# Prompt attention of one layer: scores made already turned, row maxima from rough scores ahead of them, and a new order at the edge between pairs of heads

## The reference, cut to what matters

```
q, k, v, f = split(rmsnorm(x) @ w_in)          # 16 heads of 64
q, k = rmsnorm per head (q, k); lf = log_sigmoid(f + b_f)
c = cumsum(lf)                                 # per head, over past and new frames
s = q @ k.T / 8 + c_q - c_k                    # masked to k_pos <= q_pos
attn = softmax(s) @ v                          # fp32
```

## Time and profile before

| | us |
|---|---|
| median of three runs | 2732.37 |
| the profiled execution | 2734.04 |
| its span, first to last instruction | 2732.4 |
| PE, DVE, ACT, POOL busy | 2316.4, 1336.0, 1020.5, 169.6 |
| attention: first projection to first score | 100.3 to 163.3 |
| attention: pairs 1 to 7 of 8 | 163.3 to 1018.6 |
| attention: last pair | 1018.6 to 1124.6 |

### The profile page before, as it was taken

The page is one execution under the profiler, slowest core; times in us unless marked ns, Lnnn a source line. Parts: engine busy times, 40 slices in busy tenths (PEclk is TensorE's granted clock), DMA queues, the critical chain, the costliest instruction groups (busy, mean ns, idle before and its releaser), DMA issues. The chain is left out here.

```text
span 2732.4 us, 37076 instructions
## 1 busy us (share of the span) xinstructions
PE 2316.4 (85%) x12096; PEld 1849.0 (68%) x12096; DVE 1336.0 (49%) x1639; ACT 1020.5 (37%) x1315; POOL 169.6 (6%) x175
## 2 busy tenths in 40 slices
PE   4678979898997989799899949989908999999991
PEld 2666858676776866699878849975505766666660
DVE  5345453545455453311255542212136888788874
ACT  3133222323323222211156632101106777777760
POOL 0111010101001000000011100000020000000002
PEclk9789999899989996799999979999958999999995
DMA  3210211302020110211245542133037999999986
GB/s 93 61 40 18 63 32 47 79 0 79 0 79 14 42 53 3 97 46 46 82 151 184 160 142 66 38 138 107 0 131 272 386 372 370 373 365 377 372 313 226
DMA packets 206037, 376.83 MB, mean 138 GB/s; under 512 B 19377, under 2 KB 127193, under 8 KB 205945
## 3 DMA queue, kind: packets, MB, share of 16 engines
q1 hardware_dynamic: 184776, 302.27, 32.7%
q0 software_dynamic: 17600, 61.18, 7.0%
q10 hardware_dynamic: 3584, 12.58, 1.2%
HBM read 301.60 MB, written 74.39 MB: 138 GB/s over the span
## 5 line engine op out<-in xcount | busy, mean ns | idle before, releaser
L1854 DVE TENSOR_TENSOR e_w_lo<-e_raw,e_w_hi 128x2048 fp32r<-128x2048 f32 x192 | 437.6, 2290 | 113.4 <-ACT e_w_hi L1781 101.0
L1781 ACT CAST e_w_hi<-e_raw 128x2048 fp32r<-128x2048 f32 x192 | 366.7, 1912 | 132.9 <-DMA e_raw<-w_down_e 53.5
L1154 ACT ACTIVATE probs_s<-scores,neg_max 128x256 f32<-128x256 f32 (+7 forms) x128 | 95.0, 742 | 446.4 <-DVEq L84 446.0
L1254 DVE COPY probsT<-turn_ps 128x512 f32<-128x512 f32 (+4 forms) x232 | 131.5, 567 | 249.1 <-PE turn_ps L1024 225.7
L101 PE MATMUL proj_ps<-w_qkv_hi,xh 128*128 128x384 f32 x544 | 194.5, 358 | 9.3 <-PEq L285 9.3
L1044 PEld LDWEIGHTS out_ps<-v_new,probsT 128*128 128x128 f32 x1152 | 160.1, 210 | 60.8 <-DVEq L84 44.3
L1044 PE MATMUL out_ps<-v_new,probsT 128*128 128x64 f32 x1152 | 180.6, 298 | 20.2 <-DVEq L84 19.0
L103 PE MATMUL proj_ps<-w_qkv_hi,xl 128*128 128x384 f32 x544 | 184.8, 340 | 0.0
L102 PE MATMUL proj_ps<-w_qkv_lo,xh 128*128 128x384 f32 x544 | 184.6, 339 | 0.0
L1240 DVE TENSOR_REDUCE neg_max<-scores 128x1 f32<-128x256 f32 (+7 forms) x128 | 97.0, 758 | 150.5 <-PE scores L1002 120.0
L1000 PE MATMUL scores<-qkT 65*128 65x512 f32 (+3 forms) x384 | 160.6, 532 | 5.8 <-DVEq L84 4.9
(11 more groups left out here) (363 smaller groups left out, 4967.1 us busy)
## 6 DMA issues: line engine op xcount, KB each, us to landing
e_raw<-w_gate_e SPq DMA_DIRECT2D x64, 1024.0 KB, 13.8
e_raw<-w_up_e SPq DMA_DIRECT2D x64, 1024.0 KB, 14.1
e_raw<-w_down_e SPq DMA_DIRECT2D x64, 1024.0 KB, 13.0
slot_x<-zrows POOLq DMA_DIRECT2D x48, 440.0 KB, 6.3
e_x<-slot_x SPq DMA_DIRECT2D x33, 384.0 KB, 11.1
w_qkv<-w_in SPq DMA_DIRECT2D x24, 512.0 KB, 10.0
slot_y<-e_y ACTq DMA_DIRECT2D x32, 384.0 KB, 6.2
slot_y<-zrows POOLq DMA_DIRECT2D x24, 352.0 KB, 9.6
```

The costliest lines, as they stand in the source:

```text
L1154: chain(sc.activation(probs[n % 2][:, 0:w], half(n)[:, 0:w], ACT.Exp, bias=neg_max[:, n:n + 1], accum_out=total[:, n:n + 1]), exp_ready)
L1254: chain(v.tensor_copy(probsT[q % 2][0:rows, 0:len(js) * P], turn_ps[0:rows, m % 2, 0:len(js) * P]), turn_taken[m % 2])
L1781: sc.copy(w_hi[u][:, :], w.raw[c][:, :]).then_inc(wh_ready, 1)
L1854: v.tensor_tensor(w_lo[u][:, :], w.raw[c][:, :], w_hi[u][:, :], ALU.subtract).then_inc(wl_ready, 1)
```

## The change

What it does, part by part:

- Scores of the prompt are made with keys on the partitions and 512 queries as the moving side, so they need no turning. There are four units (two heads, two halves of the queries) with 4, 8, 4 and 8 tiles of keys, together 24 steps (STEPS). A score is two fp32r matmuls into one bank: q and k rounded to fp32r, with three more rows for -c and the query's maximum (67 rows), and a second one of the two cross terms stacked to 128 rows.
- The exponential of a step is one ACT instruction of up to 512 columns straight into the moving side of the weighing. The values are stationary, with 64 columns of ones beside them, so the sum of the probabilities comes out of the same matmul on the other 64 partitions. DVE takes a reciprocal of 64x512 and one product for each unit.
- The row maximum now comes from rough scores, the first of the fp32r terms alone, in 24 chunks (MAXES) that all use one bank. PE turns the 128x3 results into rows by matmuls with the identity as the moving side, and ACT copies them behind q. The maxima of unit 0 of the next pair are taken at the edge.
- q and k are turned two tiles at a time, both heads in one transpose, in five groups. ACT writes the rounded part and a copy of k's, DVE the differences, and POOL copies q's rounded part.
- Past keys are turned for both heads at once, four times in place of eight, at steps 18 to 21. Weights are loaded and split in three parts with two raw buffers, at steps 18 and 22. The square root stands at step 19, the three parts of the normalization at 20 to 22. All of these stand ahead of the stream's scores.
- At the edge all five groups of q and k come first on every engine, then the stream's exponential, then its probabilities, with the four maximum chunks between them (EDGE).
- `forget_gates` also splits -c into two fp32r rows, and stores them with a row of ones.
- Nearly every wait inside the loops is followed by `alone`.

```diff
+    UNITS = [(0, 0), (0, 1), (1, 0), (1, 1)]
+    STEPS = [(u, j) for u in range(4) for j in range(4 * (UNITS[u][1] + 1))]
...
+    HALVES = 2 * NT
+    MAX_AT = {0: (4, 5, 6, 7), 1: (8, 9, 10, 11), 5: (12,), 6: (13,), 7: (14,), 8: (15,),
+              9: (16, 17), 10: (18, 19), 11: (20, 21), 12: (22, 23)}
+    ROWS_AT = {2: 1, 9: 2, 13: 3}
...
+    EDGE = (("qk", 0), ("qk", 1), ("qk", 2), ("qk", 3), ("qk", 4), ("p", 0), ("max", 0), ("p", 1), ("weigh", 0), ("max", 1),
+            ("weigh", 1), ("max", 2), ("p", 2), ("max", 3), ("weigh", 2), ("p", 3), ("rows", 0), ("weigh", 3), ("p", 4), ("weigh", 4))
...
+                def max_chunk(n):
+                    u, t, c0 = MAXES[n]
...
+                    last = te.matmul(max_ps[:, 0:w], high[0:HD + 2, h, 0, t * P:(t + 1) * P], high[0:HD + 2, h, 1, c0:c0 + w],
+                                     start=True, stop=not diagonal)
...
-                        for c0 in range(0, (t + 1) * P, BANK):
-                            w = min(BANK, (t + 1) * P - c0)
-                            diagonal = c0 + w == (t + 1) * P
-                            te.matmul(half(n)[:, c0:c0 + w], qkT[:, h, t * P:(t + 1) * P], qkT[:, 2 + h, c0:c0 + w],
-                                      start=True, stop=not diagonal)
...
+                        te.matmul(out[:, 0:q1 - q0], high[0:HD + 3, h, 1, j * P:(j + 1) * P], high[0:HD + 3, h, 0, q0:q1],
+                                  start=True, stop=False)
+                        last = te.matmul(out[:, 0:q1 - q0], cross[:, h, 1, j * P:(j + 1) * P], cross[:, h, 0, q0:q1],
+                                         start=False, stop=not diagonal)
...
+                        te.matmul(out_ps[u % 2][:, q0 - c * BANK:BANK], v_one[:, j, h, :], probsT[s % 2][:, 0:q1 - q0],
+                                  start=(j == 0), stop=(s == last_step(u)), skip_group_check=True).then_inc(pv_done, 1)
...
+                        def some_max():
+                            if maxes:
+                                n = maxes.pop(0)
+                                pe.wait_ge(max_taken, i * NM + n)
+                                alone(pe, g)
+                                max_chunk(n)
...
+                        some_max()
+                        some_max()
+                        if ahead and s < HALVES:
+                            project_half(s // 2, s % 2, proj_ps)
+                        some_max()
...
+                def take_cross(chain, p, b, bank):
+                    dve.wait_ge(high_ready, p * BATCHES + b + 1)
...
+                            chain(v.tensor_tensor(halves(cross[into, h, z, cols]), by_z[:, z, :, :], halves(high[0:HD, h, z, cols]),
+                                                  ALU.subtract), turn_taken[bank] if h and z else None)
...
+                        chain(v.reciprocal(recip[mine, :], out_ps[u % 2][other, :]))
+                        chain(v.tensor_tensor(out_T[mine, c * BANK:(c + 1) * BANK], out_ps[u % 2][mine, :], recip[mine, :], ALU.mult), out_taken)
```

More of the change, by code:

```diff
@@ L1101, in _ @@
+                    pe.wait_ge(out_taken, i * 5 + 5)
+                    alone(pe, g)
+                    bank = bank_of("o", 0)
+                    te.transpose(turn_ps[:, bank, 0:P], o_s, g.ident[:, :]).then_inc(turned, 1)
                 with pe.Fori(0, PAIRS - 1) as i:
@@ L1134, in _ @@
+                ones.then_inc(ones_ready, 1)
                 for t in range(NT):
[L1135 removed]
+                    take_tile(0, t, (proj_ps, out_ps[1])[t % 2], first=True)
                 root(0)
[L1137 to L1141 removed]
+                for b in range(BATCHES):
+                    act.wait_ge(turned, b + 1)
+                    alone(act, g)
+                    take_qk(b, b % 2)
@@ new lines, in past @@
+                    def past(c):
+                        m = use["past", c]
+                        act.wait_ge(turned, turned_count(i, m))
+                        alone(act, g)
+                        for h in range(2):
+                            last = sc.copy(kT_past[0:HD, h, c * BANK:(c + 1) * BANK], turn_ps[rows_of(h), m % 2, :])
+                            if h == 0:
+                                last.then_inc(chain_a, 1)
+                        last.then_inc(turn_taken[m % 2], 1)
@@ L1177, in step @@
-                    if ahead:
-                        root(i + 1)
-                        if more:
-                            round_w(i + 2)
-                        chain(sc.activation(warm[:, :], g.ident[:, 0:1], ACT.Exp))
-                        for t in range(TAKE_QK_ACT):
-                            m = use["qk", t]
-                            act.wait_ge(turned, turned_count(i, m))
-                            take_qk(chain, t, m % 2)
-                    exp(STREAM)
-                    if ahead:
-                        chain.ended(A_STEPS)
+                            alone(act, g)
@@ new lines, in step, with soft_stream @@
+                        if ahead and s == ROOT_AT:
+                            root(i + 1)
+                            sc.activation(warm[:, :], g.ident[:, 0:1], ACT.Exp).then_inc(chain_a, 1)
+                        if more and s in W_AT:
+                            for n in W_AT[s]:
+                                round_w(i + 2, n)
+                    def soft_stream():
+                        act.wait_ge(max_ready, i + 1)
+                        alone(act, g)
+                        sc.activation(probs_s, scores[:, :], ACT.Exp, bias=neg_max[:, 0:1], accum_out=total[:, 0:1]).then_inc(chain_a, 1)
+                        sc.activation(probs_tail[:, :], tail, ACT.Exp, bias=neg_max[:, 0:1], accum_out=total[:, 1:2]).then_inc(soft_ready, 1)
@@ L1191, in _ @@
+                    if not ahead:
+                        soft_stream()
+                        return
+                    for b in range(BATCHES):
+                        m = use["qk", b]
+                        act.wait_ge(turned, turned_count(i, m))
+                        alone(act, g)
+                        take_qk(b, m % 2)
+                    soft_stream()
+                    rows(0, i + 1)
                 with act.Fori(0, PAIRS - 2) as i:
@@ L1230, in _ @@
                     norm_part(chain, 0, s)
+                for b in range(BATCHES):
+                    take_cross(chain, 0, b, b % 2)
+                for n in range(U0_MAXES):
+                    maximum(chain, 0, n)
                 chain.ended(V_FIRST)
@@ new lines, in take_probs @@
+                        chain(v.tensor_copy(probsT[q % 2][0:rows, 0:n], turn_ps[0:rows, m % 2, 0:n]), turn_taken[m % 2])
+                    for s in range(NS):
+                        for n in MAX_AT.get(s, ()):
+                            maximum(chain, i, n)
+                        if s and STEPS[s - 1][0] != STEPS[s][0]:
+                            take_out(STEPS[s - 1][0])
+                        if ahead and s < HALVES and s % 2:
+                            sum_squares(chain, i + 1, s // 2)
+                        if ahead and s == HALVES - 1:
+                            mean(chain)
+                        if ahead and s in NORM_AT:
+                            norm_part(chain, i + 1, NORM_AT[s])
```

750 lines of the change are left out of this document (443 added, 307 removed).

## The result

The changed kernel took 2851.2 us (median of 4 runs, 2815.1 to 2865.1), the kernel before 2738.7 on the same chips (2718.8 to 2755.0). The ratio is 1.033 with a 95% interval of 1.018 to 1.048: slower, though the interval does not leave out a loss of under 2%. The profiled execution has a span of 2839.7 us, 107.3 more than before.

A forecast was written before the change was run, and what follows sets the result against it. The prediction took PE's work to bound the body and an ACT and DVE chain the edge. Pairs -16.5, start +7 and last pair -20 gave -29.5; from 2734.0, less 1.7 to the median, 2703 us, range 2646 to 2762.

The forecast's parts named there:

- The body, its clock: Body of each pair, up to the last projection: work priced at full clock, 73.5 us in all, against 83.3 before.
- The body, its work: PE's matmuls in a body, priced from the nearest rows of the old trace: 62.6 us.
- The body, its waits: PE's waits in a body: 7.5 for chunks sharing a bank, 0.8 for rows, 1.6 for tile copies, 1.0 for semaphores.
- The edge: From a pair's last projection to the next pair: 46.0 us, 2.5 of it for the clock, against 37.9; bounds 41 to 51.
- Six steps... ACT must clear them: At the edge's start: the last unit's six steps queue on ACT, ending near 13 us after the last projection.
- Rival 2: The edge eats the body's gain: a serial chain leaves PE at half clock; +26 us, 2758; chance 0.22.
- Rival 1: The clock holds in the pairs: edge 42, pair 115, last pair 70 us; -78 us, 2654; chance 0.27.
- Rival 3: POOL's copies hold DVE at the edge: 3.3 us a pair, 23 more than forecast, 2727; chance 0.06.
- Ahead of the pairs: Before the first score: later gates and half-clock batches, less a normalization stall; net +7 us, bounds 3 to 11.
- The last pair: Last pair of heads, without projections beneath it: 86 us instead of 106, so -20 us, bounds -42 to 0.
- Transposes and the clock: In the edge's last phase: old rows show the clock rising within transposes; by the skill's rule the edge nears 49 us.
- 2.3 us in seven pairs: Gain of each pair, 119.5 us instead of 121.8, forecast as -16.5 us over seven pairs.

The follow-up runs named there:

- e11: Changed kernel plus five useless fp32r matmuls at each of six places per body where two maximum chunks stand back to back; 2812.3 us.
- e14: e12's idea, stream's exponential after two q and k groups, third weight cast after ScalarE's first probability copy, more filler before weighings and rows; 2698.4 us, ratio 0.988.
- e2: e4 plus useless filler matmuls on TensorE in steps 21 to 23 and in the edge; 2810.7 us.
- e6: Changed kernel with maximum chunks spread through the projections, unit 3's output taken early as in e4, and e2's filler in the edge; 2732.3 us, ratio 1.001.
- e4: Changed kernel with VectorE taking unit 3's output before the stream's maxima instead of behind the subtractions; 2809.8 us.
- e8: e7 with the casts of the next weights moved out of ScalarE's queue ahead of the stream's scores; 2742.6 us, ratio 1.005.
- e12: e9 with the stream's sum of totals and its reciprocal moved behind the first copy of probabilities; 2718.3 us, ratio 0.994.
- e9: e6 with later weight casts as in e8, more filler ahead of the stream's scores, and filler in the last pair's waits; 2731.6 us, ratio 0.998.
- e7: e6 with the next pair's four maximum chunks between the q and k groups, giving up filler where they took its bank; 2754.8 us, ratio 1.012.
- e3: Changed kernel with the edge order undone: stream's exponential, probabilities and weighings first, then q and k, then maxima and rows; 2859.9 us.

## Why the prediction was wrong

- **The body, its clock: the step that failed.** "Body: 62.6 + 7.5 + 0.8 + 1.6 + 1.0 = 73.5 us" prices all at full clock. I had foretold each 1.05 us stall and asked only what it lasts, and had let the half clock of the edge end with the edge; what it costs the body stood at nothing, without a reason. Some 13 us of the second body run at half speed, half of them handed on by the edge, half from stalls on: 5 to 7 us lost, 3.9 of it shown by e11. It is one of three terms of like size. The 20.4 us by which a pair was missed are, within 0.4: this clock 6, the body's work 6.4, its waits -1.5, the edge's chain 7.7, the edge's clock 1.4.
- **The body, its work: mis-sized.** 62.6 us forecast; e14's body, at a clock of 1.00, has PE busy for 69.05. By starts of matmuls in it, projections take 40.1 (37.5 forecast), scores, masks and weighings 20.6 (18.2), chunks 5.5 (4.3), row matmuls 2.9 (2.6). The first matmul behind another kind comes after more than its pitch (0.31 us between the two halves of a score at 340.14, where 512 columns at the projections' rate give 0.23), and the new body changes kind 124 times. So rates from runs of equal matmuls came out as a lower bound for this mixed stream.
- **The body, its waits: right.** 10.9 us forecast, 9.4 measured, the 1.04 us stalls and ScalarE's tile copies among them. Sum: 69 + 9.4 + 6 = 84.4, measured 84.0 in this body.
- **The edge: mis-sized in the clock and in the chain.** "I take +2.5 of 7: edge 46.0". Measured 55.1. The clock is worth 3.9 by e2 (5.3 with what it hands to the next body, by e6). The rest is chain, read from the rows of one edge and only in parts tried by a run (e4, e8, e12): ScalarE's four casts for a batch take 1.95 us where I took 1.6, the scores start 0.9 later, and from unit 3's output to the next pair it was 15.9 us where I took 11 at full clock. "Six steps... ACT must clear them" and unit 3's reciprocal on the path were right (e4: 2.5).
- **Rival 2 was the right mechanism**, with 0.22: ScalarE's queue, half clock behind it, "at 51.5 a pair is 125". It lacked that the body pays the clock too, so even its 2758 was 93 short. Rival 1 (the clock holds) fell. Its argument, that the body had kept 0.99, read a property of the old instruction stream as one of the chip.
- **Rival 3:** the copies on GpSimd held nothing, the subtractions took 1.79 us all through. Its subtraction of two SBUF operands did: the first multiply took 1.34 us instead of 0.96 at 410.66, and e9's sum 2.25.
- **Ahead of the pairs:** +11.8 for +7. Normalization (done at 153.2 instead of 155.1) and the batches (10.9 us for 11) were right; the four maxima took 7.8 us instead of 4, four full round trips at half clock.
- **The last pair:** -19.1 for -20, right in sum by luck. I had divided 43 us of work by a clock of 0.61 and added 20 of waits, "all at full clock 64". The clock was 0.76, and at the full one the pair does not come near 64: 84.2 at 0.96 in e9 and 82.1 at 1.00 in e12, after 86.5 at 0.78 in e6. The clock is worth 2 to 4 us there, and what stands beside the 43 us of work is far more than 21.
- **Transposes and the clock:** in the kernel before, PE idled for 7.56 us and then had nothing but transposes from 391.80 on; its granted clock was 0.50 until 395.4 and 1.00 from there to 396.44. In the changed edge it rose at 448.8, among turns and weighings. The Trainium skill ("TensorE: Matmul & The Clock Gate", Part 4, PE-mode transpose) says that the full clock does not engage for transposes; these rows differ from it, and they decide.
- **Two slips that move nothing:** 2.3 us in seven pairs are 16.1 and not 16.5, and PE was busy for 89% of the old last pair, not "over 90%".

Still open: how the old last pair, with PE busy for 94.6 of 106 us, came to 0.61; e7's order with its filler kept; and where the last 0.6 us of e12's expected gain went.

## What to carry to other kernels

A wait on PE can be priced twice: as it lasts, and at half clock for what stands behind it, the next stage included. Not each one is: of the six stalls of 1.04 us in the body above, the clock fell with two. So spread the short dependent matmuls of a chain through long ones, and where a pause stays, useless matmuls into a free bank can be worth more than they cost (5.3 us a pair here, 1.2% with a better order). When a change makes one engine's work shorter and its pauses more, take no clock from the old profile.

## What was not expected of the hardware

- Pauses of 1.04 us were among those behind which PE went from 2.4 to 1.2 GHz: at 329.3, after pauses of 0.41 and 1.04 us, and at 380.5, after 0.69 and 1.04. Behind single ones of 1.04, at 364.26, 370.16 and 375.03, it did not. Filling them with five fp32r matmuls of 384 columns each brought the second body's clock from 0.92 to 0.97.
- With a clock near 1.00 pairs repeat to 0.1 us (117.25, 117.28, 117.25, 117.25, 117.29 for pairs 2 to 6 of e14); those of the changed kernel scattered by 2.6 us (138.3 to 140.9). A low clock alone does not do it: e3's pairs 2 to 6, at 0.66 or so in their edges, lie between 143.1 and 143.4.
- A VectorE operation on 128x1 elements waited for the whole of a 2.33 us GpSimd subtraction when both read two operands from SBUF. A copy out of PSUM beside the same subtraction kept its 0.69 us (GpSimd, then VectorE, in e14):

```profile
400.52 2.36 POOL L954 TENSOR_TENSOR w_qkv_lo<-w_raw,w_qkv_hi 128x1024 fp32r<-128x1024 f32 x1 [1.41 <-ACT w_qkv_hi L1287]
...
401.70 0.69 DVE L1539 COPY mT<-turn_ps 128x512 f32<-128x512 f32 x1 [1.63 <-PE turn_ps L1158]
```

  The Trainium skill ("GPSIMD Engine Reference", Specifications) puts the contention on two SBUF inputs (and two-port modes); the trace agrees. The one that comes second waits: in the changed kernel a multiply of VectorE at 416.00 kept its 0.96 us, and the subtraction that GpSimd began beside it at 416.50 took 2.66 us instead of 2.33.
